# Reordered banks, sums, first keys and transposes between the stages of a two-block transformer kernel

## What is computed

```python
x = x + expert_choice_ffn(rms_norm(x, norm_ffn), ...)
g = sigmoid(rms_norm(x, norm_ple) @ w_ple_gate)
x = x + g * rms_norm(p @ w_ple_proj, norm_ple_post)
# second block, layer 1
h = rms_norm(x, norm_g) * (1 + scale) + shift
u, v, z = split(h @ w_in, 3)                 # v first, with w_causal later
x = x + gate * ((gelu(u) * mixed * silu(z)) @ w_out)
# keys and values, then layer 2
k, v = split(h @ w_kv, 2);  k = rms_norm(k per head) * k_norm_g
q = rms_norm(q per head) * q_norm_g * 128 ** -0.5
s = q @ k - slope * distance;  softmax;  o = p @ v
```

## Time and profile before

| what | us |
|---|---|
| median of 3 runs (2017.0 to 2019.09) | 2017.27 |
| the profiled execution | 2017.61 |
| its span, first to last instruction | 2015.8 |
| TensorE busy | 1904.5 |
| VectorE busy | 831.1 |
| ScalarE busy | 569.0 |

### The profile page before, as it was taken

One profiled execution on the slowest core, in us unless ns is written; L12 is line 12 of the kernel. 1 busy time (PEld: TensorE's weight loads), 2 busy tenths in 40 slices (PEclk: granted clock), 3 DMA queues, 4 the chain that ended last, 5 costly groups with the idle time before them and its releaser, 6 DMA issues.

```text
span 2015.8 us, 22450 instructions
## 1 busy us (share of the span) xinstructions
PE 1904.5 (94%) x9037; PEld 1127.4 (56%) x9037; DVE 831.1 (41%) x1275; ACT 569.0 (28%) x901; POOL 36.9 (2%) x40
## 2 busy tenths in 40 slices
PE   7999899999999989899998999999999999999998
PEld 6667533333233323223333377888888778778877
DVE  6886511111111101111110166466566675876544
ACT  5563400000000000000000055443133433246761
POOL 1022000000000000000000000000000000000000
PEclk9999899999999999999999999999999999999999
DMA  8533699999999999999999954545244223211101
GB/s 268 209 100 118 271 383 428 429 427 429 429 427 429 429 428 429 429 428 429 428 428 429 402 197 159 187 151 191 87 167 171 81 86 102 84 42 50 56 22 42
DMA packets 105112, 528.17 MB, mean 262 GB/s; under 512 B 6998, under 2 KB 52884, under 8 KB 80340
## 3 DMA queue, kind: packets, MB, share of 16 engines
q1 hardware_dynamic: 102420, 520.55, 64.4%
q0 software_dynamic: 1008, 3.52, 0.8%
q10 hardware_dynamic: 1616, 3.15, 0.4%
HBM read 524.97 MB, written 2.23 MB: 262 GB/s over the span
## 4 chain that ended last, share of the span: by engine, by line
PE 66%; DMA 22%; DVE 7%; ACT 4%; issue 2%; ACTq 0%; DVEq 0%
DMA w_expert<-in_w_up 21%; PE bank L1219 9%; PE bank L1208 9%; PE bank L947 5%; PE bank L949 5%; PE bank L948 5%; PE bank L924 5%; PE bank L926 5%; PE bank L925 5%; PE bank L1181 3%; DVE full L1991 1%; PE bank L1229 1%; DVE w_lo L1896 1%; PE bank L1437 1%; PE bank L1406 1%
## 5 line engine op out<-in xcount | busy, mean ns | idle before, releaser
L1208 PE MATMUL bank<-w_expert,chosen 128*64 128x512 f32 x2048 | 467.7, 598 | 55.7 <-DMA w_expert<-in_w_up 40.8
L1208 PEld LDWEIGHTS bank<-w_expert,chosen 128*64 128x64 f32 x2048 | 137.6, 136 | 366.7 <-issue 277.5
L2192 DVE TENSOR_TENSOR x_res<-x_res,bank 128x512 f32<-128x512 f32 x136 | 87.1, 683 | 421.9 <-PE bank L1229 401.8
L1219 PE MATMUL bank<-w_expert,hidden_t 128*64 128x512 f32 x1024 | 226.8, 595 | 4.6 <-ACT hidden_t L1686 4.6
L1896 DVE TENSOR_TENSOR w_lo<-raw,w_hi 128x2048 fp32r<-128x2048 f32 x74 | 170.3, 2303 | 125.8 <-ACT w_hi L1484 125.7
L1484 ACT CAST w_hi<-raw 128x2048 fp32r<-128x2048 f32 x74 | 141.0, 1905 | 129.0 <-PE bank L949 122.9
L2214 DVE TENSOR_TENSOR hidden_rows<-gate_silu,bank 128x512 f32<-128x512 f32 x32 | 20.5, 683 | 346.4 <-PE bank L1208 346.4
L924 PE MATMUL bank<-act_hi,w_hi 128*128 128x512 f32 x408 | 161.5, 396 | 1.9 <-DVE q L1982 1.4
L926 PE MATMUL bank<-act_hi,w_lo 128*128 128x512 f32 x408 | 158.9, 389 | 0.0
L925 PE MATMUL bank<-act_lo,w_hi 128*128 128x512 f32 x408 | 158.8, 389 | 0.0
L1219 PEld LDWEIGHTS bank<-w_expert,hidden_t 128*64 128x64 f32 x1024 | 75.6, 137 | 132.5 <-issue 124.1
(11 more groups left out here) (326 smaller groups left out, 2563.0 us busy)
## 6 DMA issues: line engine op xcount, KB each, us to landing
w_expert<-in_w_gate SPq DMA_DIRECT2D x64, 2048.0 KB, 39.5
w_expert<-in_w_up SPq DMA_DIRECT2D x64, 2048.0 KB, 37.1
w_expert<-in_w_down SPq DMA_DIRECT2D x64, 2048.0 KB, 39.0
raw<-in_a_w_in SPq DMA_DIRECT2D x24, 1024.0 KB, 6.7
raw<-in_b_w_in SPq DMA_DIRECT2D x16, 1024.0 KB, 5.3
raw<-in_a_ada_w SPq DMA_DIRECT2D x12, 1024.0 KB, 6.7
raw<-in_b_ada_w SPq DMA_DIRECT2D x12, 1024.0 KB, 6.2
raw<-in_kv_ada_w SPq DMA_DIRECT2D x8, 1024.0 KB, 5.5
```

The lines of the kernel that those rows point to most:

```text
L1208: last = mm(PS[b0 + n][HALF[x], :], XE[:, k % 4, HALF[k // 4]], WE[place][:, c0:c0 + 512], start=(k == 0), stop=(k == KD - 1), skip_group_ ...
L1219: last = mm(PS[4][HALF[x], :], HT[:, 4 * q + k, HALF[half]], WE[place][:, c0:c0 + 512], start=(i == 0 and k == 0), stop=(i == 7 and k == 3 ...
L2192: tt(part, part, ps[:, :], ALU.add).then_inc(d_add, 1)
```

## The change

Five edits, all behind the experts.

1. Norm 2's eight chunks use four banks (0 to 3) twice. The first gate's products go chunk by chunk over four row tiles in three passes (hi·hi, hi·lo, lo·hi); the second four chunks are turned behind the first pass. `ws` stands between the gates, on banks 4 and 5, and DVE's product with it too.
2. `keep_busy` puts 30 transposes of the identity before norm 3, into its first bank. The first values after norm 3 go chunk by chunk over four banks, all begun first.
3. `norm_by_tiles` turns norm 4 tile by tile, with 10 and 4 idle transposes behind the second and third tile.
4. The first two keys are computed together, chunk by chunk. The last couples of the keys and of query group 1 are summed a chunk on; of group 2 the last two heads are summed and scaled singly.
5. Query couples get their banks by hand: 3 and 4, 6 and 7, 0 and 1 in turn, sums on 2 and 5.

```diff
+        for kc in range(KD):
+            note(("norm", 2, kc), "lo", kc % 4)
+        for t in range(NT):
+            note(("pgate", 0, t), "act", 4 + t)
         for i in range(2):
-            note(("ws", i), "dve")
+            note(("ws", i), "dve", 4 + i)
+        for t in range(NT):
+            note(("pgate", 1, t), "act", t)
+        ring[0] = 2
         note_norm(3)
...
         for g in (1, 2):
             for j in range(H2):
-                note(("q2", g, j), "head")
+                note(("q2", g, j), "head", ((3, 4), (6, 7), (0, 1))[(4 * (g - 1) + j // 2) % 3][j % 2])
+                if (g, j) == (2, 0):
+                    note(("q2ss", 1, 3), "act", 5)
                 if j in (2, 4, 6):
-                    note(("q2ss", g, j // 2 - 1), "act")
-            note(("q2ss", g, H2 // 2 - 1), "act")
+                    note(("q2ss", g, j // 2 - 1), "act", (2, 5, 2)[j // 2 - 1])
+        note(("q2ss", 2, "6"), "act", 5)
+        note(("q2ss", 2, "7"), "act", 2)
...
+            def keep_busy(key, n):
+                before_ = fills[key][4]
+                pe.wait_ge(freed[fills[before_][1]], fills[before_][2])
+                for _ in range(n):
+                    nc.tensor.transpose(bank(key)[:, 0:P], ident, ident)
+            def norm_by_tiles(k):
...
+                for t in range(NT - 1):
+                    for chunks in (range(0, 4), range(4, KD)):
+                        turn(chunks, t)
+                    if t:
+                        keep_warm(banks[0], NT - 1, 10 if t == 1 else 4)
+                for chunks in (range(0, 4), range(4, KD)):
+                    turn(chunks, NT - 1)
...
+                    if by_chunks and s == 0:
+                        banks = [begin(key, ends_next=False) for key in keys]
+                        for k in range(4):
+                            pe.wait_ge(f_lo, f0(k))
+                            for t in range(NT):
...
+            def first_gates():
+                for s in range(2):
...
+                    for n, (x, weights) in enumerate(((AH, hi), (AH, lo), (AL, hi))):
+                        if n == 1:
+                            pe.wait_ge(lo_ready, w + 1)
+                        for kc in range(4 * s, 4 * s + 4):
+                            if n != 1:
+                                pe.wait_ge(f_lo if n else f_hi, 18 + kc + 1)
+                            for t in range(NT):
...
+                        if s == 0 and n == 0:
+                            x_turned(range(4, KD))
...
+            keep_busy(("norm", 3, 0), 30)
             norm(3)
...
-            norm(4)
-            for j in range(6):
-                fm_chunk(W_K[j // 2], j % 2, ("k2", j), BH, BL, 50 if j == 0 else None)
+            norm_by_tiles(4)
...
+                banks = [begin(("k2", c), ends_next=False) for c in range(2)]
+                for kc in range(KD):
+                    pe.wait_ge(f_lo, 50 + kc + 1)
+                    for c in range(2):
...
-            pair_squares(("k2ss", 2), 8 + 4)
             for c in range(KV2):
                 fm_chunk(W_V0, c, ("vf", c), BH, BL)
+                if c == 0:
+                    pair_squares(("k2ss", 2), 8 + 4)
...
+                    if (g, j) == (2, 0):
+                        pair_squares(("q2ss", 1, 3), q_no(1, 6))
...
-                pair_squares(("q2ss", g, 3), q_no(g, 6))
+            for j in (6, 7):
+                head_squares(("q2ss", 2, str(j)), q_no(2, j), ONES[:, :])
```

More of the change, by code:

```diff
@@ L889, in ends, with turn, keep_warm @@
                 at_fill[0] += 1
+            def keep_busy(key, n):
[4 more added lines that the diff above has]
+            def norm_by_tiles(k):
+                banks = {}
+                def turn(chunks, t):
+                    pe.wait_ge(*rows_scaled(k, t, chunks[0] // 4))
+                    for kc in chunks:
+                        if t == 0:
+                            banks[kc] = begin(("norm", k, kc))
+                        last = nc.tensor.transpose(banks[kc][:, t * P:(t + 1) * P], XNORM[k][:, t, kc * P:(kc + 1) * P], ident)
+                        if t == NT - 1:
+                            last.then_inc(filled, 1)
+                for t in range(NT - 1):
[5 more added lines that the diff above has]
+                    turn(chunks, NT - 1)
+            def keep_warm(b, t, n):
+                for _ in range(n):
+                    nc.tensor.transpose(b[:, t * P:(t + 1) * P], ident, ident)
             def norm(k):
                 banks = []
-                for chunks in (range(0, 4), range(4, KD)) if k in (2, 3, 4) else (range(0, 6), range(6, KD)):
+                for chunks in (range(0, 4), range(4, KD)) if k in (3, 4) else (range(0, 6), range(6, KD)):
                     for t in range(NT):
[L896 to L899, removed]
+                        pe.wait_ge(*rows_scaled(min(k, 4), t, chunks[0] // 4))
                         for kc in chunks:
@@ L927, in fm_chunk, with tm_unit @@
                 last.then_inc(filled, 1)
-            def tm_unit(ws, keys, ah, al, f0=None, halves=(0, 1), between=None, ahead=None):
+            def tm_unit(ws, keys, ah, al, f0=None, halves=(0, 1), between=None, ahead=None, by_chunks=False):
                 banks = []
@@ L1285, in _, with x_turned @@
                        ).then_inc(m_c, 1)
-            norm(2)
-            for h in range(2):
[L1290 to L1298, removed]
+            def x_turned(chunks):
+                for t in range(NT):
+                    pe.wait_ge(d_add, ADDS - 8 + max(4, 2 * t + 2))
+                    for kc in chunks:
+                        b = begin(("norm", 2, kc)) if t == 0 else bank(("norm", 2, kc))
+                        last = nc.tensor.transpose(b[:, t * P:(t + 1) * P], X[:, t, kc * P:(kc + 1) * P], ident)
+                        if t == NT - 1:
+                            last.then_inc(filled, 1)
@@ new lines, in first_gates @@
+            def first_gates():
+                banks = []
+                for s in range(2):
+                    w = W_PGATE[0][s]
+                    hi, lo = w_hi(w), w_lo(w)
+                    pe.wait_ge(hi_ready, w + 1)
+                    for n, (x, weights) in enumerate(((AH, hi), (AH, lo), (AL, hi))):
[4 more added lines that the diff above has]
+                                pe.wait_ge(f_lo if n else f_hi, 18 + kc + 1)
+                            for t in range(NT):
+                                key = ("pgate", 0, t)
+                                if s == 0 and n == 0 and kc == 0:
+                                    banks.append(begin(key, ends_next=False))
+                                last = mm(banks[t][:, :], x[:, kc, t * P:(t + 1) * P], weights[:, kc % 4 * 512:(kc % 4 + 1) * 512],
+                                          start=(s == 0 and n == 0 and kc == 0), stop=(n == 2 and kc == KD - 1))
+                                if n == 2 and kc == KD - 1:
+                                    ends(key)
+                                    last.then_inc(filled, 1)
+                        if s == 0 and n == 0:
+                            x_turned(range(4, KD))
+                    if s == 0:
+                        last.then_inc(half_used, 1)
@@ new lines, in _ @@
+            x_turned(range(0, 4))
+            for h in range(2):
+                if h == 0:
+                    first_gates()
+                else:
+                    tm_unit(W_PGATE[h], [("pgate", h, t) for t in range(NT)], AH, AL)
+                if h == 0:
+                    pe.wait_ge(s_ws, 16)
+                    for i in range(2):
+                        b = begin(("ws", i))
+                        for g in range(4):
+                            last = nc.tensor.transpose(b[:, g * P:(g + 1) * P], WS_IN[:, 4 * i + g, :], ident)
+                        last.then_inc(filled, 1)
@@ L1299, in _ @@
+            keep_busy(("norm", 3, 0), 30)
             norm(3)
             for h in range(4):
-                tm_unit(W_AV[h], [("av", h, t) for t in range(NT)], AH, AL, from_lo(26) if h == 0 else None)
+                tm_unit(W_AV[h], [("av", h, t) for t in range(NT)], AH, AL, from_lo(26) if h == 0 else None, by_chunks=(h == 0))
                 if h == 1:
@@ L1539, in split_hi, with norm_hi @@
                 f[0] += 1
-            def norm_hi(k):
-                for kc in range(KD):
+            def norm_hi(k, chunks=range(KD)):
+                for kc in chunks:
                     split_hi(("norm", k, kc), AH[:, kc, :], mul=NORM_MUL[k](kc))
@@ L2232, in _ @@
                 split_upto(W_PGATE[h][1] + 1)
+                if h == 1:
+                    dve.wait_ge(s_late, 32)
+                    ts(QGS, QGS, QG2, None, ALU.mult).then_inc(s_cols, 1)
+                    tril = CL[:, 4 * P:5 * P]
+                    for i in range(2):
+                        b = take(("ws", i))
+                        tt(WST[:, 4 * i:4 * i + 4, :], b[:, :].rearrange("p (g t) -> p g t", g=4), repeat(tril, 4),
```

(1 more changed line is left out.)

58 lines of the change are left out of this document (37 added, 21 removed).

## The result

The changed kernel takes 2022.92 us (median of 17 runs, 2018.59 to 2025.1), the kernel before 2018.55 in the same series (17 runs, 2015.24 to 2020.89): a ratio of 1.0023, 95% interval 1.0016 to 1.0029. It is slower by 4.4 us, where no change was forecast, and lies 1.4 us above the top of the range. The forecast started from the 2017.27 of three runs; in this series the kernel before itself stands 1.3 us higher, so that much of the distance is not the change's.

What follows compares the result with a forecast made beforehand. TensorE, busy for 94% of the span, was taken as the bound, with the experts fed by DMA. Terms summed to -1.5 us; clock additions of 1.2 and 0.3 made 0.0, so 2017.5 us, range 2012.5 to 2021.5.

Steps and rivals of the forecast that it cites:

- term 1: Behind the experts, norm 2's chunks in two fours let the first gate's products start sooner: -0.2 us.
- term 2: Between the gates, the spatial weights' turns stand on the path and wait for two banks: +1.3 us.
- Term 3: At norm 3, idle turns cost nothing, but first values chunk by chunk wait for four banks: +0.5 us, between 0 and +0.9.
- Terms 4 and 5: Norm 4 by tiles with two keys together: -2.8 us; last couples' squares a chunk later: -1.4; weights in time: -0.5.
- Term 6: First query chunk, its bank now placed by hand, waits for ACT's copy of v0 from bank 3: +4.3 us.
- Term 7: End of queries: single heads bring scores 3.5 us sooner, VectorE takes part back; first probabilities: -2.7 us, between 0 and -3.5.
- term 5: Keys and first query group: last couples' squares a chunk later, -1.4 us; next weights split in time, -0.5.
- the clock: Added to the terms: 1.2 us for one fall behind the bank 3 stall, and 0.3 for norm 3.
- Rival B: Slower: idles before the gates' values, keys and first probabilities each bring a clock fall onto products: +4.9 us, 2022.4; chance 0.13.
- Rival A: Faster: no wait for bank 3 before the first query chunk, so 4.3 and 1.2 us fall away: 2012.0; chance 0.15.
- C: Turns don't hold the clock: norm 4 falls as before, keys start at half clock: 2019.6 us; chance 0.10.
- D: VectorE becomes the bound in the second attention's first heads, so the query-end gain is nothing: 2020.2 us; chance 0.10.

Runs made afterwards that it cites:

- the filled kernel: The changed kernel with more idle turns in four gaps (before first values, first keys, first query chunk, first probabilities), waits unchanged: 2016.23 us, ratio 0.9991.
- the shifted kernels: The changed kernel with value tiles' banks placed by hand, plus 8 or 16 idle turns ahead of the third key chunk: single runs of 2015.66 and 2016.22 us.
- the fastest kernel: The changed kernel with value banks, first values tile by tile, spatial weights behind the second gate, and remaining gaps filled with idle turns: 2009.98 us, ratio 0.9962.
- the second experiment: The changed kernel with 16, 14, 38 and 20 idle turns added before first values, first keys, first query chunk and first probabilities: 2016.23 us, ratio 0.9991.
- the last mended kernel: The changed kernel with value banks, values by tiles, spatial weights behind the second gate, 40 idle turns before norm 3, other gaps filled: 2009.98 us.

## Why the prediction was wrong

**Terms 1 and 2.** The gates are 1.39 us longer (1.1 forecast). Without the moved spatial weights they take what they took before (50.76 + 3.59 = 54.35 against 54.36), so term 1 gave 0 and not -0.2, and term 2 is 1.38 (1.3).

**Term 3** was right in its wait: the first value product stands 6.06 us behind norm 3's first turn (forecast 0.85 more than 5.13, measured 0.93), with ACT's fourth pass as what ends last. The clock after it was the error: 0.3 was put there, 1.56 is what filling the gap gave back. I also missed that by_chunks costs 1.0 us once norm 3's turns run at full clock (27.94 against 26.95).

**Terms 4 and 5** were right: -2.63 for -2.8, -0.72 for -0.7, and no last couple waits on a square. Norm 4 kept the clock.

**Term 6** was right in its wait (4.7 less 0.4 against 4.3). The fall behind it was priced at one of 1.2; it lasts 7 us and costs 2.6.

**Term 7** was right to 0.5 us: -5.42 to the scores for -4.7 (with the rest of term 5), then +1.01 for +0.8. But the gap before the first probabilities, 2.54 us of idleness, brought a fall of 1.6 where none was in the sum.

**The step that failed is the clock**: +1.5 for one fall and a fifth of another, where filling the gaps shows three that cost 5.7. The waits and moves came to -1.5 in the forecast and to -1.7 by the filled kernel. Two choices made the error: the price of a fall was set by what filled it in the trace of before (turns, half-empty stretches), at 1.2, though the prediction itself has 1.7 where products fill it, and falls were counted by the longest gap alone. Rival B named two of the three places (values and probabilities; not the keys, which fell only without idle turns and in one of the shifted kernels) and their price of 1.7; it stood at 0.13. That its 2022.4 lies near the 2022.92 is in part luck: it stands on the forecast's 1.2 for the fall at the bank, asks for three more falls and got two, and what is missing came from that 1.2 being 2.6 and from the kernel before standing higher. The prediction had named half clock in the first values as a sign of being wrong, and it is there. The three gaps were all in my working, each with its length; I did not ask of each what stands behind it.

Rival A fell by the 4.46 us at L960; C by norm 4, which kept the clock, and by the run without idle turns; D by the first probabilities, which came 4.4 us nearer to the queries' first 72 products, of which term 5 has only 1.2, with nothing given back behind them.

What stays open is why one and the same gap brings a fall in one profile and none in another. How often each did can be counted over the profiles: behind 4.46 us before the first query chunk in 5 of 5, behind 2.35 before the first values in 4 of 4, behind 2.5 before the first probabilities in 8 of 10, behind 1.93 before norm 3's turns in 3 of 9, behind 1.94 before the first keys in 2 of 10, behind 1.67 before the last head's combination in 1 of 12. Over all executions the mean granted clock fits that: 0.9916 in the 17 of the changed kernel and 0.9957 in the 11 with its gaps filled. That is 8 us of full clock, give or take 3, where the windows of the three falls shown above miss 6.4. So the falls are not the profiled execution's alone. The medians' distances from the kernel before agree with those of the profiled stages to 1.9 us or better (7.3 and 8.5 us in the fastest kernel, 1.9 and 0.1 in the second experiment), which is about one fall.

## What to carry to other kernels

Price an idle stretch of TensorE of 2 us or more by its length and by what runs behind it: here a fall cost 1.6 us (2.6 behind 4.5 us of idleness) where products filled it, and 0.2 to 0.9 where it lay on turns and products that wait for ACT and VectorE anyway. Idle turns that fill a gap must stand ahead of the wait and last to its end; with some 2 us left open behind them the clock still fell in 3 of 9 profiles, and in the changed kernel the next gap brought its own fall. Before a bank is placed by hand, list for each bank when its last reader is done, not only in which order the fills come.

## What the runs showed of the hardware

Turns alone held the upper clock: in the last mended kernel TensorE did nothing but turns from 1212.57 to 1221.08, every window there at 1.00 and each turn 0.11 us. In all profiles, every fall between the first turn behind the experts and the last 2 us of the execution began inside an idle stretch of TensorE of 1.67 us or more, or within 1.3 us behind its end. The same idle stretch of 2.5 us brought a fall in one kernel and none in the same one shifted by 0.86 us, and identical code fell at different gaps from one kernel to the next. So one profile shows which gaps can bring a fall, not what they cost on average.
